# Stores and first loads moved over three stage seams of a two-layer encoder kernel

## The reference, cut to what matters

```python
h = rms_norm(x, norm_w) * (1 + scale) + shift      # scale, shift, gate from silu(c) @ ada_w
z = h @ w_in
z_a = centred_conv3(z[..., :A_CONV_COLS], conv_a)  # features: r, k, v, low-rank decay and rate
g_a, c_q, c_kv, k_rope, g_b, u_c, v_c, g_c = split(z[..., A_CONV_COLS:])
y_a = rwkv7_branch(...)      # scan over tokens in both directions, group norm, * silu(g_a)
y_b = mla_branch(...)        # six heads of attention, * silu(g_b)
y_c = sgu_branch(...)        # u_c * (w_s @ layer_norm(v_c) + b_s) * silu(g_c)
x = x + gate * (concat(y_a, y_b, y_c) @ w_out)
```

## Time and profile before

| what | value |
|---|---|
| median of three runs | 5346.09 us (5344.9 to 5358.3) |
| the profiled execution | 5354.03 us, its span 5352.2 us |
| granted TensorE clock, mean | 0.98 of full |
| PE busy | 5077.7 us, 95% of the span |
| DVE busy | 2813.2 us, 53% |
| ACT busy | 2091.1 us, 39% |
| POOL busy | 512.8 us, 10% |
| DMA, mean | 125 GB/s |

### The profile page before, as it was taken

One profiled execution on the slowest core, in us unless ns is written; L12 is line 12 of the kernel. 1 busy time (PEld: TensorE's weight loads), 2 busy tenths in 40 slices (PEclk: granted clock), 3 DMA queues, 4 the chain that ended last, 5 costly groups with the idle time before them and its releaser, 6 DMA issues. The chain is left out here.

```text
span 5352.2 us, 97775 instructions
## 1 busy us (share of the span) xinstructions
PE 5077.7 (95%) x40460; PEld 2651.1 (50%) x40460; DVE 2813.2 (53%) x4438; ACT 2091.1 (39%) x3590; POOL 512.8 (10%) x950
## 2 busy tenths in 40 slices
PE   8999999989979999989989999999899799999899
PEld 3444344467764444444444443444678544444454
DVE  2222377646555555556522223876466455655565
ACT  1121455345545444521111214553456444444211
POOL 0000000033320000001100000000333200000011
PEclk9999999999989999999999999999999899999899
DMA  6311566456651222136343115664656502221353
GB/s 228 141 69 53 193 204 212 143 164 165 168 132 26 50 57 53 37 122 219 120 165 142 69 55 189 212 204 145 169 161 172 131 20 58 57 45 37 116 177 113
DMA packets 549653, 668.51 MB, mean 125 GB/s; under 512 B 200976, under 2 KB 427792, under 8 KB 539168
## 3 DMA queue, kind: packets, MB, share of 16 engines
q1 hardware_dynamic: 548624, 661.17, 39.7%
q10 hardware_dynamic: 592, 1.10, 0.1%
HBM read 395.01 MB, written 267.13 MB: 124 GB/s over the span
## 5 line engine op out<-in xcount | busy, mean ns | idle before, releaser
L490 PE MATMUL ps<-feat_hT,w_features 128*128 128x512 f32 x2240 | 974.2, 593 | 0.0
L810 PE MATMUL ps<-w_tokens,prep_hT 128*128 128x512 f32 (+1 forms) x1920 | 822.0, 588 | 21.8 <-DMA prep_hT<-s_ht 21.8
L490 PEld LDWEIGHTS ps<-feat_hT,w_features 128*128 128x128 f32 x2240 | 421.0, 190 | 507.1 <-issue 504.0
L1889 DVE TENSOR_REDUCE att_mx<-ps 128x1 f32<-128x1024 f32 x384 | 453.4, 1220 | 282.5 <-PE ps L1765 280.6
L810 PEld LDWEIGHTS ps<-w_tokens,prep_hT 128*128 128x128 f32 x1920 | 363.7, 191 | 468.8 <-issue 441.5
L2170 PE MATMUL ps<-w_out,fin_yT 128*128 128x512 f32 x1280 | 569.5, 598 | 2.5 <-DVE fin_yT L2120 2.5
L1784 PEld LDWEIGHTS ps<-kc,att_pr 128*128 128x128 f32 x3264 | 350.9, 140 | 322.8 <-issue 275.8
L1853 ACT ACTIVATE att_PT<-ps 128x512 f32<-128x512 f32 x384 | 229.1, 597 | 631.3 <-PE ps L1784 628.2
L1784 PE MATMUL ps<-kc,att_pr 128*128 128x128 f32 x3264 | 456.5, 280 | 5.9 <-ACT att_PT L1853 2.7
L1844 ACT ACTIVATE att_pr<-ps,att_nb 128x1024 f32<-128x1024 f32 x384 | 424.6, 1110 | 68.5 <-DVE att_nb L1891 68.4
L1898 DVE COPY att_PT<-ps 128x512 f32<-128x512 f32 x384 | 264.1, 688 | 284.9 <-PE ps L1784 284.9
(11 more groups left out here) (232 smaller groups left out, 6788.8 us busy)
## 6 DMA issues: line engine op xcount, KB each, us to landing
s_sc<-prep_sc SPq DMA_DIRECT2D x20, 3072.0 KB, 9.0
scan_src<-s_sc SPq DMA_DIRECT2D x160, 384.0 KB, 4.9
s_qkt<-scan_qT SPq DMA_DIRECT2D x40, 576.0 KB
fin_z<-s_zt SPq DMA_DIRECT2D x40, 576.0 KB, 5.2
s_zf<-feat_co SPq DMA_DIRECT2D x88, 256.0 KB, 2.6
s_ht<-feat_hT SPq DMA_DIRECT2D x10, 2048.0 KB, 7.9
prep_hT<-s_ht SPq DMA_DIRECT2D x40, 512.0 KB, 5.8
s_zt<-prep_st SPq DMA_DIRECT2D x80, 256.0 KB, 3.5
```

Source lines behind the costliest of these rows:

```text
L490: last = pe.matmul(b, wf[:, k, i * P:(i + 1) * P], hT[g % 2][:, k, :], start=(k == 0), stop=(k == KD - 1))
L810: last = pe.matmul(ps[:, tiles.bank(pieces[n]), 0:c1 - c0], hT[j % NH][:, k, :], wt[:, k, c0:c1], start=(k == 0), stop=(k == KD - 1))
L1889: ch.link(v.tensor_reduce(mx[:, n % 2, half:half + 1], ps[:, 2 * half:2 * half + 2, :].rearrange("p b n -> p (b n)"), AX.X, ALU.max))
```

## The change

- **Tiles that outlive a stage.** `st`, `go_z`, `src0` and `xc0` are opened around the first three stages of a layer, and reused in turn: `src0` is the feature stage's x, then `rk_in[0]` (with `norm` and `rkb` behind it), then the scan's first rows. `qk`, `oa0` and `odd_out` are opened around attention and out.
- **Seam A.** The last group of `feature_projection` loads `hT0` after its `ht` store. The stage no longer waits for the gate pieces; the last `load_gate` of the token stage and its first `solve` do.
- **Seam B.** The end of `token_projection` on SP is reordered: after the last inverse stores come the scan's first z and rope rows, its first rows (six transfers), store 58, the wait for the inverses, the scan's first blocks (eight transfers), store 59. The wait for the pieces is gone; the scan's last `load_z` has it.
- **Seam C.** After the last head's scores, SP issues eight loads for out's tile 0 (`load_tile0`): both halves of oa, z, x, both gate tables of group 0, and the two residual gates. All count on one semaphore, `tile0_in`. The last head's store has a semaphore of its own, which only out's `load_heads(0)` waits for. In out, tile 0 goes in the order `sv, yc, ya, yb`, DVE gates b last, and SP starts with tile 1.
- Two semaphore names go from the feature stage, three from the token stage, one from out.

```diff
@@ build
+                st = tail.enter_context(nc.sbuf_tensor(f"st{l}", [P, 3, 512], F32))
...
+                src0 = tail.enter_context(nc.sbuf_tensor(f"src0_{l}", [P, TPG * D], F32))
+                xc0 = tail.enter_context(nc.sbuf_tensor(f"xc0_{l}", [P, 2 * G], F32))
@@ feature_projection, SP
                     if g + 1 < NG:
                         load_x(g + 1)
+                    else:
+                        sp.wait_ge(kept[0], 16)
+                        sp.dma_start(hT0[:, :, :], d["ht"][:, 0:P].rearrange("(k p) t -> p k t", p=P)).then_inc(h0_in, 16)
...
                 for g in range(2):
                     sp.wait_ge(kept[g], 16 * len(range(g, NG, 2)))
-                    sp.wait_ge(g_sent[g], 16 * len(range(g, BA * NG, 2)))
@@ token_projection, SP
+                    if g == NG - 1:
+                        for n in range(2):
+                            sp.wait_ge(gate_piece_sent[n], 16 * (l + 1) * len(range(n, BA * NG, 2)))
...
-                load_h(0)
                 load_rk(0)
                 load_low(0)
...
                 store_inverse(NG - 1)
-                for n in range(len(pieces) - 2, len(pieces)):
-                    store_piece(n)
-                for i in range(NB):
-                    sp.wait_ge(piece_sent[i], 16 * len(range(i, len(pieces), NB)))
+                for n in range(PT):
+                    sp.wait_ge(piece_sent[n % NB], pieces_sent(n % NB, 1))
+                sp.dma_start(zb[:, 0, :], d["zt"][0:P, 0:Z_GB]).then_inc(z0_in, 16)
+                sp.dma_start(rope[:, 0, :], d["rope"][0:P, :]).then_inc(z0_in, 16)
+                for e in range(2):
+                    sp.wait_ge(dir_sent[e], 16 * 2 * NG)
+                scan_rows(sp, d, 0, step0[0], rows0_in)
+                store_piece(len(pieces) - 2)
+                sp.wait_ge(x_sent, 16 * 2 * NG)
+                sp.wait_ge(xt_sent, 16 * 2 * NG)
+                scan_blocks(sp, d, 0, step0[1], blocks0_in)
+                store_piece(len(pieces) - 1)
@@ scan_rows and scan_blocks are the bodies of the scan's load_rows and load_blocks; rwkv_scan, SP
+                    if q == NT - 1:
+                        for n in range(3):
+                            sp.wait_ge(piece_sent[n], 16 * (l + 1) * NT)
...
-                load_rows(0)
-                load_z(0)
-                load_blocks(0)
                 sp.dma_start(pend[:, :, :], d["pe"].rearrange("(m p) t -> p m t", p=P)).then_inc(ends_in, 16)
@@ mla_attention, SP
+                def load_tile0():
+                    oa0, z0, x0, gn, bn, gate = tile0
+                    for e in range(2):
+                        sp.dma_start(oa0[:, e, :], d["oa"][e * T:e * T + P, :]).then_inc(tile0_in, 16)
+                    sp.dma_start(z0, d["zt"][0:P, Z_GB:WT]).then_inc(tile0_in, 16)
+                    sp.dma_start(x0, (d["x"] if l == 0 else d["xs"])[0:P, :]).then_inc(tile0_in, 16)
+                    sp.dma_start(gn, d["gn"][:, 0:G].rearrange("(m p) t -> p m t", p=P)).then_inc(tile0_in, 16)
+                    sp.dma_start(bn, d["bn"][:, 0:G].rearrange("(m p) t -> p m t", p=P)).then_inc(tile0_in, 16)
+                    for s in range(2):
+                        sp.dma_start(gate[:, s, :], d["gate"][s:s + 1, :].to_broadcast([P, D])).then_inc(tile0_in, 16)
...
+                    if h == HB - 1:
+                        sp.wait_ge(scored, 4 * NSLOT * HB)
+                        load_tile0()
                     sp.wait_ge(normed, GROUPS * (h + 1))
...
-                sp.wait_ge(sent1, 16 * (HB // 2))
+                sp.wait_ge(sent1, 16 * (HB // 2 - 1))
@@ out_projection
-            order += [("sv", 0), ("yb", 0), ("yc", 0), ("ya", 0)]
+            order += [("sv", 0), ("yc", 0), ("ya", 0), ("yb", 0)]
...
-                load(0)
-                load_gates(0)
-                for s in range(2):
-                    sp.dma_start(gate[:, s, :], d["gate"][s:s + 1, :].to_broadcast([P, D])).then_inc(gate_in, 16)
-                for n in range(1, TPG):
-                    load(n)
+                load_own(1)
+                sp.wait_ge(last_head_sent, 16 * (l + 1))
+                load_heads(0)
+                load_heads(1)
+                for n in range(2, TPG):
+                    load_own(n)
+                    load_heads(n)
...
                 variance(0)
-                gate_b(0)
                 gate_c(0)
                 normalise(0)
                 turn_a(0)
+                gate_b(0)
```

More of the change, by code:

```diff
@@ L999, in _, with scan_tile, scan_rows, scan_blocks @@
                 solve(NG - 1)
-def rwkv_scan(l, nc, d, ps, kc, col, amod, eps, ident):
+def scan_tile(q, e):
+    return q if e == 0 else NT - 1 - q
+def scan_rows(sp, d, q, src, arrived):
+    toks = [slice(scan_tile(q, e) * P, (scan_tile(q, e) + 1) * P) for e in range(2)]
+    for e in range(2):
+        for p in range(2):
+            at = (2 * scan_tile(q, e) + p) * SCW
+            sp.dma_start(src[:, e, :, 6 * p:6 * p + 4, :].rearrange("p m k t -> p m (k t)"),
+                         d["sc"][e * P:(e + 1) * P, at:at + SCW].rearrange("p (m k) -> p m k", m=BA)).then_inc(arrived, 16)
+    for e in range(2):
+        sp.dma_start(src[:, e, :, 4:6, :].rearrange("p m k t -> p m (k t)"), d["zf"][2 * BA * P:3 * BA * P, toks[e].start + 2:toks[e].stop + 2].rearrange("(m p) t -> p m t", p=P)).then_inc(arrived, 16)
+def scan_blocks(sp, d, q, xc, arrived):
+    for s in range(2):
+        for p in range(2):
+            e = p ^ s
+            t0 = scan_tile(q, e) * P + CH * p
+            for kind in range(2):
+                rows = ((kind * 2 + e) * NG + t0 // G) * BA * (G // SUB)
+                blocks = d["xi"][rows:rows + BA * (G // SUB), :].rearrange("(q n) (i c) -> (n i) q c", q=BA, i=SUB)
+                sp.dma_start(xc[slice(CH * p, CH * p + CH), kind, s, :].rearrange("p (q c) -> p q c", q=BA), blocks[t0 % G:t0 % G + CH, :, :]).then_inc(arrived, 16)
+def rwkv_scan(l, piece_sent, zb, rope, z0_in, step0, rows0_in, blocks0_in, nc, d, ps, kc, col, amod, eps, ident):
     NH2 = 2 * HB
@@ L1090, in rwkv_scan @@
         Y = sb("Y", [P, HA, SUB])
-        xc = [sb(f"xc{n}", [P, 2, 2, HA * SUB]) for n in range(2)]
+        xc = [step0[1], sb("xc1", [P, 2, 2, HA * SUB])]
         kv = [sb(f"kv{n}", [P, 2, HA, CH]) for n in range(2)]
@@ L1649, in mla_attention @@
         Vs = [sb(f"V{b}", [P, NT, DV + 1]) for b in range(2)]
-        outs = [sb(f"out{b}", [P, NT, DV]) for b in range(2)]
+        outs = [sb("out0", [P, NT, DV]), odd_out]
         pr = sb("pr", [P, 2, 4 * G])
@@ L1982, in wait_for, with wait_own @@
                 eng.wait_ge(emptied[name], n)
+            def wait_own(eng, n):
+                if n == 0:
+                    eng.wait_ge(tile0_in, 16 * 8 * (l + 1))
+                else:
+                    eng.wait_ge(arrived[n % TPG], 48 * (n // TPG + (n % TPG > 0)))
             def here(n):
@@ L1989, in _, with load_own @@
             def _(sp):
-                def load(n):
+                def load_own(n):
                     b = n % TPG
@@ L2039, in _ @@
                     a.activation(oa[b][:, 1, :], oa[b][:, 0, :], ACT.Square, scale=DH ** -0.5).then_inc(squared, 1)
-                    turned_out(("yb", n))
-                    turned_out(("yc", n))
+                    for name in ("yb", "yc") if n else ("yc", "yb"):
+                        turned_out((name, n))
             @block.gpsimd
```

176 lines of the change are left out of this document (100 added, 76 removed).

## The result

Four executions of the kernel after took 5310.96 to 5321.72 us, with a median of 5318.35; four of the kernel before, 5344.9 to 5358.3, median 5349.32. The ratio is 0.9933, 95% interval [0.9921, 0.9945]. In a second comparison side by side, six executions after (median 5311.43) against eleven before (5344.45) gave 0.9936 [0.9921, 0.9951]. So the change is worth 31 us by the first medians and 33 by the second; 39.6 were forecast, and the first median lies 11.9 us above the forecast of 5306.5. It is inside the stated range (5294 to 5324) and outside the band to which the forecast gave 0.70 (5299 to 5313); the second median lies within that band. The profiled execution took 5310.96 us.

What follows compares the result with a forecast made beforehand. PE was taken to bound the kernel, busy 5077.7 of 5352.2 us, with losses in scan dependences and seams. 2 x (3.8 + 8.5 + 7.5) = 39.6 us off the 5346.09 us median gave 5306.5, range 5294 to 5324.

Steps and rivals of the forecast that it cites:

- Seam A: Feature stage to token stage: earlier opening and earlier h(0) load gain 3.8 us, range 1 to 5.2.
- Seam B: Token stage to scan: PE finds its first rows loaded and gains 8.5 us, range 6.6 to 9.1.
- Seam C: Attention to out: the first product starts 7.5 us earlier, range 6 to 9.
- the second rival: At the stage closes: the close itself waits for what is in flight; gain 26 us, 5320 us; chance 0.07.
- If the load again takes 8.27 us: Token stage's r and k feature load: squares ready at 561.7, a gain of 3.9 us against 565.65.
- the second estimate: Token stage's opening: h(0) no longer ahead saves 1.3 us, squares at 560.4, a gain of 5.2 us.
- The expected hole of 1 to 2 us: Token stage, after PE's first piece: PE idles 1 to 2 us until ACT's squares end.
- Close 3.1 - 0.2: the scan opens at 1080.2, as before: Token stage's end: SP's issues fill the time of the store's landing, so the scan opens no earlier.
- PE finds its rows and starts at once: Scan's start: PE begins at the opening instead of at 1089.30, a gain of 9.1 us.
- The first rival: All six seams: a started stage cannot run at once, engines fetching code; costs 15 us, 5321 us; chance 0.14.
- The third: Out's start: tile 0's loads land late, kernel 16 us slower, chance 0.02; smaller loss, 5325 to 5335, 0.04.
- the fourth: Behind the seams: slack of the scan or token stage hides the waits again, no gain; chance 0.03.

## Why the prediction was right, and where its sizes were off

**The close stays, and takes what was read.** From the end of SP's last issue to the next stage it is 3.50 us at A (545.14 to 548.64; 3.94 in layer 1, where the kernel before has 3.9 by the same reckoning), 3.01 at B (1073.70 to 1076.71) and 1.90 at C, against 3.4, 2.9 and 1.9. At A and B the last store was still on its way to memory as the close began. At C it was so even when the close ended: the head's store lands 4.8 us after its issue, at 4982.0, and out opens at 4979.49. So the second rival, a close that waits for what is in flight, is out. The price of a name, 0.06 us, was confirmed by adding forty (0.068).

**Seam A: right mechanism, term too small.** 3.8 was put down, 5.4 and 5.0 measured. The opening was right to 0.1 us (4.44 us after the start of the last eviction; 550.0 less 545.66 makes 4.3), PE's start too. The failed step is "If the load again takes 8.27 us": without h(0) ahead of it, it took 6.62 (548.64 to 555.26), even less than the 6.97 of the second estimate, and the squares were ready as PE ended the piece. The expected hole of 1 to 2 us is missing in the first profile, because there the piece took 9.96 us instead of 9.5, at a low clock; in the second, where the piece took about 8.5, it is 1.62 and 1.67 us, ended by ACT's squares, as foreseen. I had two estimates and leaned to the slower one for the clock's sake; the rows favoured the other. Taking h(0) back into the stage cost 2.1 to 2.3 us; the other 3 stay.

**Seam B: term too large, by more than half.** 8.5 was put down; 4.4 and 4.0 measured at the turning, 3.7 and 3.2 at the state product; even the lower bound, 6.6, was too high. Two steps failed. "Close 3.1 - 0.2: the scan opens at 1080.2, as before": from the M stores to the end of the last issue I counted 10.9 us (1066.37 to 1077.3), it took 14.2. z cost 1.80 us instead of 0.5, rope 0.85, store 58 0.88 instead of 0.34, the blocks 5.63 instead of 5.33. I had priced each issue by a row in which it stood elsewhere in the queue, none of them right behind the inverse stores; the kernel with z ahead shows that what stands there pays, z or rows. I had named the blocks as the unknown, but not the instructions between. Second, "PE finds its rows and starts at once": it found its rows, and then waited for `zeroed`, which DVE's three memsets release 1.4 us after the opening. Before, that wait lay inside the wait for the rows and no row showed it; the code did. Moving it gave back its 1.4 us. And "behind it the chain is as before" left out the clock: it makes 3.7 and 3.2 us at the state product out of 4.4 and 4.0 at the turning in the first profile, and 5.4 and 3.6 out of 4.7 and 4.5 in the second. The Trainium skill (DMA: Bandwidth & Descriptors, "Queues, rings and completion order") has descriptors of one queue consumed in ring order on each DMA engine; from it the prediction took that loads issued later don't hold up the stores. The trace agrees for one queue, to 0.4 us (the M stores land in 3.9 to 5.2 us, against 3.9 to 4.8), and B was still not 9.1 us: the rule is about landing, and the time went in issuing.

**Seam C: right.** 7.5 was put down, 7.3 and 7.5 measured, through the chain as foreseen: from the opening to the product 11.97 us in layer 1 (4979.52 to 4991.49) against 12.0. The b rows, forecast to be in 7 us after the opening, came after 9.2 to 9.4: the head's store, which their load waits for, landed 4.8 us after its issue instead of 3.7, and the two loads behind it (4981.99) landed after 6.7 to 6.9 us. DVE takes gate b at 4989.31, without a pause behind the line before it, so there was room for 0.4 to 0.6 us. In layer 0 there was none: issued at 2325.96 and landing after 7.3 to 7.5 us, they came as DVE took gate b (2333.39), and the product is 0.1 us later than in layer 1. The term held by a hair.

**The sum.** 2 x (3.8 + 8.5 + 7.5) = 39.6 against 32.1 measured in the six seams. The errors of A and B are of opposite sign, 2.8 us too little and 10.1 too much, and C is 0.2 off. The median fell within the range because it reached to the rivals and two errors partly cancelled; the number was in part luck. Two of the rivals came out near the measured median (5321, 5320) for reasons that weren't theirs: at 5318.35, a time alone would not have told a late start of the engines or a waiting close from an issue chain. The first rival, code fetched late, is not seen: in all three seams the first instruction of PE or DVE comes 0.03 to 0.2 us after SP's where no wait stands before it (548.82, 4979.52, and 1077.23 with `zeroed` moved). What that rival's price was taken from, the hole of 3.90 us inside the scan, does go with the fetching of instructions; it just doesn't fall on the seams. The third and the fourth (tile 0 late; nothing gained) are out by the rows of seam C.

**The signs.** Three that were named came: the first L810 within 0.3 us of its stage (0.18), C's product 14 us after the last store (14.27, released by ACT), and A's hole, though not in the first profile. Two didn't: L1494 came 1.4 us after the scan opened, and the scan opened 9.7 us after the last token product's start instead of within 1 us of the 6.3 before. None of the signs for a wrong mechanism came.

**What stays open.** The scan stage varied from 475 to 489 us in the twelve profiles of the kernel after and its variants, with the same program but for its start. The "issue" holes make most of that: they sum to 14 to 26 us in a scan. Whether the shared queues make it longer in layer 0, or chance does, the runs don't tell: the two kernels with shared queues have 25 to 26 us of such holes there, but a kernel with one queue (the three products) has 24.5, and the unchanged kernel took 486.5 us for the scan of layer 1 in its second profile. Nor is it shown why a fetch comes late, or why the clock rises sooner in one execution than in the next.

## What to carry to other kernels

When transfers are moved ahead of a close, price each issue by rows in which it stands behind the same transfers, not by rows from another place in the queue, and count the issuing queue as a stage of its own: here the store's landing was hidden and 3 us of issuing took its place. When a long wait is removed, read in the code every other wait at that instruction; the profile names only the last. Read a seam in more than one profile before calling two ends simultaneous: one slow spell of the clock can hide which of them is the limit. And when a seam has been cut, look at the clock behind it: a few products that nobody needs were worth 1.2 to 1.4 us here, about as much as the loads moved before them.

## What the runs showed of the hardware

- The issue of z's load took SP 0.37 us ahead of the inverse stores and 1.80 us right behind them; the six row loads took 5.65 us in that place (the longest 1.85) and 3.17 behind z and rope.
- Stores that landed 3.9 to 5.2 us after their issue with loads behind them in the same queue landed after 5.8 to 7.9 us with loads fed by another queue, some of them issued ahead of the stores.
- Three products of 2.81 us in a stage's close kept the granted clock at 1.00; without them it was 0.63 from 549 to 553 us in the kernel with the same loads, 0.50 and 0.65 in the two profiles of the kernel after.
- A semaphore name costs 0.068 us at the close of its stage.
- PE's holes without a releaser inside the scan end 1.2 to 1.7 us after a 16 KB packet of the instruction queue, in all 331 cases over 0.5 us.
- From its first norm product to its last product the token stage took 508.2 us in every profile, the scan stage 475 to 489: on one core, the difference between executions of a kernel lies in some of its stages only.
